# FFN 2's gate and up: one whole pair of tiles instead of two, and another order at the start of the blocks

## The reference

```
h = modulate(rms_norm(x, norm_ffn2), sh3, sc3)            # 512 x 1024
x = x + 0.5 * g3 * (silu(h @ w_gate) * (h @ w_up)) @ w_down   # w_gate, w_up: 1024 x 2816
```

## Time and profile before

| | us |
|---|---|
| median of three runs | 1157.45 |
| profiled execution | 1155.71 |
| its span, first to last instruction | 1153.6 |
| tensor engine busy | 1132.6 (98%) |
| vector engine busy | 737.0 (64%) |
| scalar engine busy | 493.1 (43%) |
| GpSimd busy | 117.8 (10%) |

### The profile page before, as it was taken

One profiled execution on the slowest core, in us unless ns is written; L12 is line 12 of the kernel. 1 busy time (PEld: TensorE's weight loads), 2 busy tenths in 40 slices (PEclk: granted clock), 3 DMA queues, 4 the chain that ended last, 5 costly groups with the idle time before them and its releaser, 6 DMA issues. The chain is left out here.

```text
span 1153.6 us, 17468 instructions
## 1 busy us (share of the span) xinstructions
PE 1132.6 (98%) x6378; PEld 989.6 (86%) x6378; DVE 737.0 (64%) x1167; ACT 493.1 (43%) x758; POOL 117.8 (10%) x115
## 2 busy tenths in 40 slices
PE   8999999999999999999999999999989999999997
PEld 6788888888888998888888888889889999978887
DVE  4766665666555666675555666757789898952332
ACT  5233332233222257665555665533545454532232
POOL 3301000000110001112011230001310101100000
PEclk9999999999999999999999999999999999999999
DMA  9567566557777425538246674341335445333331
GB/s 311 166 214 248 186 216 203 170 175 233 230 235 237 121 59 119 121 101 171 73 121 118 141 144 98 90 128 56 105 101 145 126 128 147 111 101 91 96 114 73
DMA packets 244174, 167.95 MB, mean 146 GB/s; under 512 B 6198, under 2 KB 224516, under 8 KB 244116
## 3 DMA queue, kind: packets, MB, share of 16 engines
q1 hardware_dynamic: 227188, 143.48, 41.6%
q0 software_dynamic: 16208, 21.33, 8.8%
q10 hardware_dynamic: 720, 2.36, 0.6%
HBM read 164.99 MB, written 16.05 MB: 157 GB/s over the span
## 5 line engine op out<-in xcount | busy, mean ns | idle before, releaser
L1893 PE MATMUL bank<-hH,wH 128*128 128x512 f32 (+1 forms) x976 | 355.1, 364 | 3.9 <-DVE hL L1283 3.4
L1895 PE MATMUL bank<-hH,wL 128*128 128x512 f32 (+1 forms) x976 | 351.2, 360 | 0.0
L1894 PE MATMUL bank<-hL,wH 128*128 128x512 f32 (+1 forms) x976 | 351.0, 360 | 0.0
L798 ACT ACTIVATE wH<-raw 128x1024 fp32r<-128x1024 f32 x131 | 135.8, 1037 | 351.2 <-PE bank L1895 348.4
L1217 DVE TENSOR_TENSOR wL<-raw,wH 128x1024 fp32r<-128x1024 f32 x131 | 156.7, 1196 | 201.3 <-ACT wH L798 200.4
L1893 PEld LDWEIGHTS bank<-hH,wH 128*128 128x128 f32 x976 | 184.1, 189 | 33.6 <-issue 5.4
L1895 PEld LDWEIGHTS bank<-hH,wL 128*128 128x128 f32 x976 | 184.0, 189 | 28.0
L1894 PEld LDWEIGHTS bank<-hL,wH 128*128 128x128 f32 x976 | 184.2, 189 | 26.3
L1893 PE MATMUL bank<-actH,wH 128*128 128x512 f32 (+1 forms) x316 | 120.7, 382 | 0.0
L1895 PE MATMUL bank<-actH,wL 128*128 128x512 f32 (+1 forms) x316 | 120.4, 381 | 0.0
L1894 PE MATMUL bank<-actL,wH 128*128 128x512 f32 (+1 forms) x316 | 120.4, 381 | 0.0
(11 more groups left out here) (276 smaller groups left out, 1932.6 us busy)
## 6 DMA issues: line engine op xcount, KB each, us to landing
adaw<-in_ada_w_dram SPq DMA_DIRECT2D x28, 1024.0 KB, 6.1
raw<-in_mix_w_in_dram SPq DMA_DIRECT2D x41, 512.0 KB, 3.9
raw<-in_ffn_w_down_dram SPq DMA_DIRECT2D x32, 512.0 KB, 4.0
raw<-in_ffn_w_gate_dram SPq DMA_DIRECT2D x25, 512.0 KB, 4.0
raw<-in_ffn_w_up_dram SPq DMA_DIRECT2D x25, 512.0 KB, 3.9
adas<-in_ada_w_dram SPq DMA_DIRECT2D x16, 512.0 KB, 8.2
raw<-in_ffn_w_down_dram SPq DMA_DIRECT2D x16, 384.0 KB, 4.2
wsum_d<-in_ffn_w_gate_dram POOLq DMA_DIRECT2D x8, 704.0 KB, 7.7
```

The costliest lines, as they stand in the source:

```text
L798: nc.scalar.activation(wH[s][:, :n * P], raw[s][:, :n * P], ACT.Copy).then_inc(hi_done, 1)
L1893: T.matmul(o, a[0], b[0], start=start, stop=False)
L1894: T.matmul(o, a[0], b[1], start=False, stop=False)
L1895: return T.matmul(o, a[1], b[0], start=False, stop=stop)
```

## The change

`DIRECT` goes from 2 to 1: the second pair is done by blocks too, as the first of now ten rounds, and its four whole units (with their weights' loads and splits, silu, product and split of the result) go. The start of the blocks is written in another order on GpSimd, ScalarE and VectorE. GpSimd makes the blocks in the order 11, 12, 21, 22, each behind a wait of its own: 11 and 21 once the first half of the tokens is normalised, 12 once tiles 0 to 3 of the second half are, 22 once all are.

```diff
-    HF, DIRECT = FT // 2, 2
+    HF, DIRECT = FT // 2, 1
...
+    WHOLE = (11, 12, 21, 22)
...
             def whole(n):
-                q = (12, 11, 22, 21)[n]
+                q = WHOLE[n]
+                pool.wait_ge(hL_done, (4 + q % 10 - 1) * DT - (DT // 2 if q == 12 else 0))
                 nc.gpsimd.tensor_tensor(hB[q][:, :, :], f32(block_of(hH, q)), f32(block_of(hL, q)), ALU.add).then_inc(h_whole, 1)
...
                 if n == 4:
-                    pool.wait_ge(hL_done, 5 * DT)
                     for q in range(4):
                         whole(q)
... (scalar engine)
-                for j in range(2):
-                    prep_home(u0 + N_FIRST + j, u0 + (1, N_FIRST)[j])
-                    silu(0, 2 * j)
+                w_high(0)
+                silu(0, 0)
+                silu(0, 2)
+                w_high(1)
+                t_high(5, 1)
                 for j in range(2):
                     hi(0, j)
-                prep(u0, 4, 1, 2)
-                silu(1, 0)
-                prep(u0, 4, 1, 3)
-                hi(1, 0)
                 t_high(6, 3)
                 t_high(7, 2)
                 t_high(4, 4)
-                w_high(0)
-                silu(1, 2)
-                w_high(1)
-                t_high(5, 1)
-                hi(1, 1)
                 for t in range(N_TWOS):
                     two_by_blocks(t)
... (vector engine; token_sums(0) and (1) are cut anew into t1 and t_others)
+            def t1():
+                dve.wait_ge(h_whole, 2)
+                V.tensor_tensor(hB[11][:, :, :], hB[11][:, :, :], hB[12][:, :, :], ALU.subtract).then_inc(t_sum, 1)
+            def t_others():
+                b = {q: t[:, :, :] for q, t in hB.items()}
+                dve.wait_ge(h_whole, 4)
+                dve.wait_ge(t_sum, 1)
+                V.tensor_tensor(b[12], b[22], b[12], ALU.subtract).then_inc(t_sum, 1)
+                dve.wait_ge(t_sum, 2)
+                V.scalar_tensor_tensor(out=b[22], in0=b[22], scalar=-1.0, in1=b[11], op0=ALU.mult, op1=ALU.subtract).then_inc(t_sum, 1)
+                dve.wait_ge(t_sum, 3)
+                V.scalar_tensor_tensor(out=b[21], in0=b[22], scalar=-1.0, in1=b[21], op0=ALU.mult, op1=ALU.subtract).then_inc(t_sum, 1)
...
-                for j in range(2):
-                    prep_home(u0 + N_FIRST + j)
-                    product(0, j)
+                t1()
+                w_low(0)
+                product(0, 0)
+                t_others()
+                product(0, 1)
+                w_low(1)
+                t_low(5, 1)
                 for j in range(2):
                     lo(0, j)
-                prep(u0, 4, 1, 2)
-                token_sums(0)
-                product(1, 0)
-                prep(u0, 4, 1, 3)
-                lo(1, 0)
-                token_sums(1)
-                t_low(6, 1)
-                t_low(7, 2)
-                t_low(4, 3)
-                w_low(0)
-                w_low(1)
-                t_low(5, 4)
-                product(1, 1)
-                lo(1, 1)
+                t_low(6, 2)
+                t_low(7, 3)
+                t_low(4, 4)
... (tensor engine)
-                u0 = U_GU2
-                for k in range(4):
-                    pe.wait_ge((silu_done, prod_done)[k % 2][1][k // 2], 1 + START)
-                    h_unit(4 + u0 + k, (u0 + k) % 2, bank[:, k, :]).then_inc(unit_done, 1)
...
-                        pe.wait_ge(t_lo, {6: 1, 7: 2, 4: 3, 5: 4}[p])
+                        pe.wait_ge(t_lo, {5: 1, 6: 2, 7: 3, 4: 4}[p])
```

More of the change, by code:

```diff
@@ L1444, in t_low @@
                 V.tensor_tensor(l, hB[{6: 22, 7: 12, 4: 21, 5: 11}[p]][:, :, :], f32(h), ALU.subtract).then_inc(t_lo, 1)
-            def token_sums(n):
+            def t1():
+                dve.wait_ge(h_whole, 2)
+                V.tensor_tensor(hB[11][:, :, :], hB[11][:, :, :], hB[12][:, :, :], ALU.subtract).then_inc(t_sum, 1)
+            def t_others():
                 b = {q: t[:, :, :] for q, t in hB.items()}
[L1449 to L1460, removed]
+                dve.wait_ge(h_whole, 4)
[5 more added lines that the diff above has]
+                V.scalar_tensor_tensor(out=b[21], in0=b[22], scalar=-1.0, in1=b[21], op0=ALU.mult, op1=ALU.subtract).then_inc(t_sum, 1)
             def act_low(t, j):
```

## The result

The changed kernel took 1171.68 us, the median of four runs (1167.98 to 1174.61), against 1157.49 for the old one: ratio 1.012, interval 1.0097 to 1.0143. In a second set, beside the experiments, it took 1172.22 against 1157.23: ratio 1.0138, interval 1.0121 to 1.0155. So it is slower by 14 to 15 us. Forecast were 1168 and a range of 1162 to 1173: the measured median lies in the range, 3.7 above the forecast, and nearest to the 1171 of the second rival. Its profiled execution was the fastest of its set: 1167.98 us, with a span of 1166.3.

A forecast was written before the change was run, and what follows sets the result against it. The tensor engine bounds the rounds, a chain over other engines the start of the blocks. -1.75 - 4.65 + 14.55 + 2.3 = +10.45 us gives 1166.2 profiled; the median, 1.7 above, 1168, range 1162 to 1173.

The forecast's parts named there:

- second rival: Start of the blocks: GpSimd collisions and the low clock cost more, +13 to +15 us, so 1171; chance 0.18.
- Seven products for eight: Second pair: four whole units of 21.79 us give way to a round of 20.04 us, a gain of 1.75 us.
- The old waits removed: Old first round: 4.65 us over a round without waits, about 3.05 idle and 1.6 slow product 5, go.
- The chain behind E: New first round: uncovered sums, splits and a load delay products; second round at 34.6 in place of 20.04, costing 14.55 us.
- E: End of the first pair's whole units, 811.94 us in the old trace; forecast to come 2.3 us later.
- The early halves: Third norm's second half: GpSimd's early block sums hold up vector engine operations, moving E 2.3 us later.
- the 1.4 us that the prediction left out: First silu's table load: the skill's drain of about 1.38 us per table switch, not counted in the forecast.
- The sum: Whole kernel: -1.75 - 4.65 + 14.55 + 2.3 = +10.45 us, so 1166.2 profiled and 1168 as median.

The follow-up runs named there:

- old_again: The old kernel once more, with no edit; 1157.87 us (1156.88 to 1162.85).
- again: The changed kernel once more, with no edit; 1172.22 us (1170.85 to 1174.50), 15.0 over the old kernel.
- early_load: Changed kernel, but product 5's weights are loaded into a free place, without waiting for the third t_low; 1166.08 us, ratio 1.0073 to the old kernel.
- old_early_halves: Old kernel with only GpSimd's part of the change, each block sum made as soon as its halves are there; 1160.12 us, ratio 1.0026.
- late_halves: Changed kernel, but all four GpSimd block sums wait until the whole norm is done; 1170.26 us, ratio 1.0116 to the old kernel.
- act_sums: Changed kernel, but the scalar engine makes the four block sums in place of GpSimd; 1166.21 us, ratio 1.0076 to the old kernel.

## Why the prediction was right, step by step

- *Seven products for eight, -1.75.* The rounds behind the first are 20.05 us long in the changed kernel too. Right for a round without waits; old_again and again have later rounds that wait for 0.2 to 0.5. It is a difference of two rows, and no experiment took it apart.
- *The old waits removed, -4.65.* Right for the trace that I read. In old_again product 5 took 3.62 in place of 4.44, with a wait of 2.63 in place of 2.89 ahead of it and the granted clock at 1.00 throughout, and its first round cost only 65.99 - 20.58 - 21.79 - 20.04 = 3.58 more than one without waits. So this term varies by 1.1 between executions of the old kernel.
- *The chain behind E, 14.55.* The steps came out one by one: product 1 at E + 1.20 (forecast 1.1), product 2 at E + 7.96 (7.9), SP's load at E + 12.5 (12.6), the split of its weights at E + 16.2 (16.2), product 5 at E + 18.65 (18.7), the second round at E + 34.89 (34.6). Product 5 took 4.85 (4.44), in again 5.79 with a wait of 0.81 behind it. Sum: 14.85 and 15.97. early_load shows that the load behind t_lo is 3.7 of it. The silu began 1.29 behind the start of its table load here too (816.05 and 817.34), so the 1.4 us that the prediction left out didn't show.
- *The early halves, 2.3.* 2.80 in the trace, 2.78 in old_early_halves, where nothing else is changed, and 0 in late_halves and act_sums. Shown. It was line 1255 (old 1261) that was caught, not line 1264. The diagonal came 1.0 later (forecast 0.9), the low parts made the other 1.8 (1.4). The Trainium skill's rule ("SBUF - State Buffer", "Who interferes with whom") holds here, in both directions: the vector engine's 0.16 became 2.38 behind GpSimd, and GpSimd's 2.38 became 3.30 behind next_r.
- *The sum.* By the traces the stretch from M to the second round costs 78.33 - 67.08 = 11.25 us more, or 12.35 with again's trace, against a forecast of 10.45. The rival of a dearer lock and clock (+13 to +15) has its part in that: the clock for product 5, and in again the meeting of next_r and the weight sum. E moved by less than its 3 to 4.7.
- *The 14 to 15 of the medians.* The traces don't lead all the way. 1.4 and 2.1 us lie ahead of M, where the first old trace was early. From M to the end of the span the old kernel's two traces took 362.3 and 363.3, the changed kernel's two 373.6 and 376.1: 10.3 to 13.8 more, by which pair is taken. What is missing up to 14 or 15 stays open. The same holds for early_load and act_sums, whose medians are 6 and 7 us better than again's, and whose traces gain 4.2 to 5.3 and 1.5 to 2.6 up to the second round. Single traces can't settle this. So the mechanism is shown step by step, but that the time lay in the range owes something to the range's width: the forecast of +10.45 was 3.7 short of the medians, and the terms above account for 0.8 of that (1.9 with again's trace).
- The step that was wrong is one of reasoning, without effect on the number: I held that the early halves could win nothing. late_halves shows that without them product 1 would have waited 4.88 us. They win about as much as they cost, within the 2 us that late_halves leaves open.

## What to carry to other kernels

Before taking work away from the engine that is the bound, list what was hidden behind it on the other engines, in their order: here 21.79 us of whole units covered a chain of 18.7 us, and a change that was worth 1.75 us took them away. A sum moved to GpSimd is not beside the vector engine's work if both read two inputs from SBUF, and a tiny operation on the critical chain pays the most for its length: 2.38 us in place of 0.16. The scalar engine did the same sums without moving E. With the load's place, the sums and the lists put right for the missing cover, ten rounds beat the old kernel by 0.2%; whether nine rounds with the same remedies would do better was not run.

## What the runs showed of the hardware

An operation of 2 columns was held for 2.2 us behind a GpSimd sum that had started 0.02 us earlier, in the changed kernel. And the granted clock at the start of the program differs between executions of the same instructions. In early_load's trace it was low between 40 and 55 us, where all others had 1.00 and their low stretch between 20 and 30 us (windows, tensor engine: length, busy, granted clock, DMA):

```profile
40.00:45.00 5.00, 3.80 (x18) 0.79 0.74 190
45.00:50.00 5.00, 5.00 (x22) 0.50 0.00 0
50.00:55.00 5.00, 5.00 (x19) 0.69 0.00 0
```

That execution reached M at 796.64, 3.9 us later than the changed kernel's, with the same instructions ahead of M. That all of the 3.9 us come from the clock isn't shown. But a profile of one execution carries such an offset, and a fixed point like M takes it out.
